# Hybrid encoder block on eight cores: another order of the first stages, loads that are held back, and value products that don't wait for their gelus

## What is computed

```
h = rms_norm(x);  lru_x, lru_gate, q, k, v = split(h @ w_in)      # five blocks of 512 columns
lru_x = causal_dwconv(lru_x, width 4)
r, i  = sigmoid(block_diag(lru_x)), sigmoid(block_diag(lru_x))
a     = exp(-8 r softplus(-lambda));  u = sqrt(1 - a^2) * (i * lru_x)
out_a = gelu(lru_gate) * scan(a, u)                               # scan along the positions
out_b = per head: rms_norm((softmax(q1 k1) - lam softmax(q2 k2)) @ v)   # block-causal, 4 heads
x     = x + concat(out_a, out_b) @ w_out
gate, val = split(rms_norm(x) @ ffn_w_up)                         # 2 x 3072 columns
x     = x + (gelu(causal_dwconv(gate, width 3)) * val) @ ffn_w_down
out   = rms_norm(x)
```

## Time and profile before

| | before |
|---|---|
| median of 3 runs | 1791.77 us (1791.51 to 1796.46) |
| the profiled execution | 1792.87 us, of which the slowest core's span is 1791.2 us |
| spans of the eight cores | 1778.5 to 1791.2 us |
| mean granted TensorE clock of the cores | 0.993 to 0.997 |
| PE busy, fills included | 1729.8 us, 97% of the span |
| DVE, ACT, POOL busy | 67%, 60%, 24% |
| fills in PE's list | 274 |

### The profile page before, as it was taken

One profiled execution on the slowest core, in us unless ns is written; L12 is line 12 of the kernel. 1 busy time (PEld: TensorE's weight loads), 2 busy tenths in 40 slices (PEclk: granted clock), 3 DMA queues, 4 the chain that ended last, 5 costly groups with the idle time before them and its releaser, 6 DMA issues.

```text
span 1791.2 us, 32281 instructions; the slowest of 8 cores (1778.5 to 1791.2 us)
## 1 busy us (share of the span) xinstructions
PE 1729.8 (97%) x9714; PEld 812.6 (45%) x9714; DVE 1193.2 (67%) x2049; ACT 1068.5 (60%) x1384; POOL 426.0 (24%) x631
## 2 busy tenths in 40 slices
PE   9988899999999999999999999999999999999997
PEld 4434344444444444444444444444444444454443
DVE  3498766562788585666986486866857378656844
ACT  6788764344877576654764376546766468742811
POOL 2272442210432131111511031111312033101300
PEclk9999999999999999999999999999999999999999
DMA  9980589773437835468558846585456644245633
GB/s 284 295 257 22 164 279 292 248 212 117 150 125 239 242 98 183 132 213 259 184 182 249 244 128 203 172 246 184 131 206 203 200 166 155 87 164 183 223 141 141
DMA packets 165417, 340.54 MB, mean 190 GB/s; under 512 B 73600, under 2 KB 73856, under 8 KB 165120
## 3 DMA queue, kind: packets, MB, share of 16 engines
q1 hardware_dynamic: 165248, 338.49, 59.7%
HBM read 267.14 MB, written 55.57 MB: 180 GB/s over the span
## 4 chain that ended last, share of the span: by engine, by line
PE 76%; DMA 6%; issue 6%; DVE 4%; ACT 4%; POOL 2%; SPq 1%; DVEq 0%; ACTq 0%; POOLq 0%
PE pb L865 40%; PE pb L883 24%; PE pb L1113 6%; PE pb L1080 4%; DMA slot<-x 3%; PE pb L718 1%; DMA KT<-w_up 1%; ACT raw L956 1%; DMA slot<-w_up 1%; ACT PT L1102 1%; POOL sm L851 1%; DMA Va<-w_down 1%; POOL raw L952 1%; DMA Va<-w_in 1%; DVE aT L973 0%
## 5 line engine op out<-in xcount | busy, mean ns | idle before, releaser
L865 PE MATMUL pb<-hT,slot 128*128 128x512 bf16 x3584 | 821.5, 379 | 8.5 <-ACT raw L956 4.8
L865 PEld LDWEIGHTS pb<-hT,slot 128*128 128x128 bf16 x3584 | 335.2, 98 | 421.5 <-issue 47.9
L1102 ACT ACTIVATE PT<-pb,prm 128x1024 bf16<-128x1024 f32 (+1 forms) x288 | 306.1, 1063 | 185.4 <-PE pb L1080 82.7
L883 PE MATMUL pb<-slot,aT 128*128 128x512 bf16 x1632 | 375.8, 380 | 3.5 <-DVE slot L1226 2.1
L883 PEld LDWEIGHTS pb<-slot,aT 128*128 128x128 bf16 x1632 | 154.5, 98 | 194.8 <-issue 20.2
L851 POOL TENSOR_TENSOR sm<-sm 128x1 f32<-128x1 f32 (+1 forms) x128 | 101.2, 793 | 552.6 <-DVE sm L848 550.7
L1226 DVE TENSOR_TENSOR slot<-pb,slot 128x512 f32<-128x512 f32 x192 | 130.7, 688 | 127.0 <-PE pb L883 126.2
L1216 DVE TENSOR_TENSOR aT<-pb,aT 128x512 bf16<-128x512 f32 x192 | 131.8, 688 | 119.9 <-PE pb L865 119.1
L1113 PEld LDWEIGHTS pb<-Va,PT 128*128 128x128 bf16 x2176 | 142.9, 98 | 75.7 <-issue 26.3
L1113 PE MATMUL pb<-Va,PT 128*128 128x129 bf16 x2176 | 171.3, 221 | 5.8 <-ACT PT L1102 5.5
L973 DVE SCALAR_TENSOR_TENSOR facc<-raw,prm,facc 128x512 f32<-128x512 f32 x192 | 144.2, 755 | 27.8 <-ACT facc L967 21.7
(11 more groups left out here) (133 smaller groups left out, 1671.6 us busy)
## 6 DMA issues: line engine op xcount, KB each, us to landing
slot<-wslab SPq DMA_DIRECT2D x326, 512.0 KB, 4.7
slot<-x SPq DMA_DIRECT2D x80, 512.0 KB, 6.9
wslab<-slot SPq DMA_DIRECT2D x50, 512.0 KB, 6.1
out<-slot SPq DMA_DIRECT2D x32, 512.0 KB, 5.1
x<-slot SPq DMA_DIRECT2D x24, 512.0 KB, 3.0
KT<-w_up SPq DMA_DIRECT2D x20, 512.0 KB, 8.0
Va<-w_up SPq DMA_DIRECT2D x20, 512.0 KB, 7.6
KT<-w_in SPq DMA_DIRECT2D x10, 512.0 KB, 9.7
```

Of the source, the lines that this page charges most:

```text
L865: last = e.matmul(bank(p), lhsT=w[:, kk, cc * 128:(cc + 1) * 128], rhs=src[:, hf * 4 + kk, :], start=(hf == 0 and kk == 0), stop=(hf == 1 ...
L883: last = e.matmul(bank(p), lhsT=src[:, k0 + hf * 4 + kk, t * 128:(t + 1) * 128], rhs=w[:, kk, :], start=(hf == 0 and kk == 0), stop=(hf == ...
L1102: op("act", act_us(2 * N, ptr=1), lambda e, s=s, pt=pt, N=N, h=h: e.activation(out=PT[:, pt.s, :, 0:N], in_=psum[:, s.s:s.s + 2, 0:N], fun ...
```

## The change

The first stages of groups 0 and 1 stand in another order: V, gate, LRU of group 0, Q, K instead of Q, K, V (stage A) with the gate and then the LRU. Stage A is split into `stage_Q`, `stage_K` and `stage_V`, and `pair` gives group 1's part of each its own offset in priority. The x tiles of group 1 are no longer loaded first but as part of stage N of group 1, behind (`behind=`) the second x tile of group 0. A new number `ahead` keeps a DMA from being placed in the list earlier than 6 modelled us before the DMA queue is free for it. The write-backs of the first weight slabs get a later priority. The value products of groups 0 and 7 lose their `after`, so that they may be placed ahead of the gelu (DVE's multiplication still reads the gelu's result). The numbers in the tables are new as well, those of the later groups included.

```diff
-        bw = 290e3
+        bw, ahead = 290e3, policy.get("ahead", 1e9)
...
+                    if n.dma and t < dma_free - ahead:
+                        t = dma_free - ahead
...
-        x0 = [[load_x(x_d, gi, t, ("XF", "X")[gi], pri=-8 + 2.12 * gi) for t in range(NT)] for gi in range(NP)]
+        x0 = [[load_x(x_d, 0, t, "XF", pri=-8 if t < 2 else -6.712) for t in range(NT)], []]
...
+                if gi == 1:
+                    x0[1].append(load_x(x_d, 1, t, "X", behind=behind))
...
-                p = mm_fm(sl, i, hT2, b_hT2, after=[b_aT[a]])
+                p = mm_fm(sl, i, hT2, b_hT2, after=[] if gi in (0, 7) else [b_aT[a]])
...
-                n.pri = period + f0 + (f1 - f0) * cum / tot
+                n.pri = period + f0 + (f1 - f0) * cum / tot + (0.6 if n.tag == "wb" and period < 2 else 0.0)
...
-        PR.update({'N0': (-6.483, -6.38), 'N1': (-6.091, -6.088), 'A': (-5.838, -5.301), 'G0': (-6.221, -6.266), 'L0': (-5.302, -4.564), 'L1': (-4.817, -3.395), 'B0': (-5.395, -4.633), 'B1': (-4.505, -3.624), 'C': (-4.474, -2.824)})
+        PR.update({'N0': (-6.384, -6.4), 'N1': (-6.361, -5.827), 'V': (-6.565, -6.864, 0.202), 'G': (-6.342, -6.558, 0.638), 'L0': (-6.114, -5.643), 'Q': (-6.112, -6.035, 0.428), 'K': (-5.9, -5.767, 0.741), 'L1': (-4.919, -3.721), 'B0': (-5.951, -5.545), 'B1': (-4.702, -3.5), 'C': (-4.573, -2.567)})
...
+        def pair(name, f, *args):
...
+                if n.grp == 1:
+                    n.pri += PR[name][2]
...
+        paced(0, *PR["N1"], stage_N, 1, [x0[0][1].ld])
+        pair("V", stage_V, *both)
+        pair("G", stage_G, both, (), "g0")
         paced(0, *PR["L0"], stage_L, 0)
+        pair("Q", stage_Q, *both)
+        pair("K", stage_K, *both)
...
-        S_.schedule({"attn": attn, "slots": slots, "warm": (idle, 0.8),
+        S_.schedule({"attn": attn, "slots": slots, "warm": (idle, 0.8), "ahead": 6.0,
```

More of the change, by code:

```diff
@@ L662, in build @@
         node({"sp": 0.1}, lambda e: e.dma_start(out=stg_v()[:, 128:nst], in_=stg_d[:, 128:nst]), reads=[stg_vt],
-             writes=[b_stg2], dma=(nst - 128) * 512, tag="stg", pri=-4.99)
+             writes=[b_stg2], dma=(nst - 128) * 512, tag="stg", pri=-6.472, behind=[x0[0][1].ld])
         node({"sp": 0.1}, lambda e: e.dma_start(out=prm[:, nsmall:npar], in_=par_d[:, nsmall:npar]), writes=[b_prmb],
-             dma=(npar - nsmall) * 512, tag="prm", pri=-4.5)
+             dma=(npar - nsmall) * 512, tag="prm", pri=-5.836, behind=[x0[0][1].ld])
         op("pool", 0.6, lambda e: e.memset(smv("mhalf"), -0.5), writes=[b_sm["mhalf"]])
@@ L888, in mm_tm @@
             for hf in range(2):
-                op("pe", MMC / 2, part(hf), reads=[slabs[hf][0]] + b_src, writes=[p], tag=tag,
+                p.pe = op("pe", MMC / 2, part(hf), reads=[slabs[hf][0]] + b_src, writes=[p], tag=tag,
                    after=after if hf == 0 else (), soft=list(soft) + [slabs[1][0].ld])
@@ L921, in stage_A, with stage_Q @@
                 op("pool", 0.6, lambda e: e.memset(Va[:, 12:16, :, 128:130], 1.0), writes=[b_stg1] + b_V[12:16])
-            stg = {2: [b_stg], 3: [b_stg1]}.get(gi, [])
-            sl = [load_slab(("in", 2, hf), "A", pr) for hf in range(2)]
+            stage_Q(gi)
+            stage_K(gi)
+            stage_V(gi)
+        def stage_Q(*gis):
+            S_.grp = gis[0]
+            sl = [load_slab(("in", 2, hf), "A", S_.pri) for hf in range(2)]
             for gi in gis:
                 S_.grp = gi
+                stg = claims(gi)
                 hT, b_hT, qT_, b_qT_ = place(gi)[:4]
@@ L929, in stage_A, with stage_K @@
                     evac(p, (lambda h=h: qT_()[:, h, :]) if gi == 1 else qT[:, h, :], b_qT_[h], scale=0.125, stg=stg)
-            S_.grp = 0
-            sl = [load_slab(("in", 3, hf), "A", pr) for hf in range(2)]
+        def stage_K(*gis):
+            S_.grp = gis[0]
+            sl = [load_slab(("in", 3, hf), "A", S_.pri) for hf in range(2)]
             for gi in gis:
                 S_.grp = gi
+                stg = claims(gi)
                 hT, b_hT = place(gi)[:2]
@@ L938, in stage_A, with stage_V @@
                     evac(p, KT[:, g, h, :], b_KT[h][g], stg=stg)
-            S_.grp = 0
-            sl = [load_slab(("in", 4, hf), "A", pr) for hf in range(2)]
+        def stage_V(*gis):
+            S_.grp = gis[0]
+            sl = [load_slab(("in", 4, hf), "A", S_.pri) for hf in range(2)]
             for gi in gis:
                 S_.grp = gi
+                stg = claims(gi)
                 hT, b_hT = place(gi)[:2]
@@ L1046, in stage_G @@
         def stage_G(gis, behind=(), visit=None):
-            pr = S_.pri
-            sl = [load_slab(("in", 1, hf), "F" if gis[0] == 0 else "A", pr) for hf in range(2)]
+            S_.grp = gis[0]
+            sl = [load_slab(("in", 1, hf), "F" if gis[0] == 0 else "A", S_.pri) for hf in range(2)]
             for gi, c in itertools.product(gis, range(4)):
@@ L1329, in build @@
         paced(0, *PR["N0"], stage_N, 0)
-        paced(0, *PR["N1"], stage_N, 1)
-        i0 = len(S_.nodes)
-        paced(0, *PR["A"], stage_A, *both)
-        for n in S_.nodes[i0:]:
-            if n.grp == 1:
-                n.pri += 0.772
-        i0 = len(S_.nodes)
-        paced(0, *PR["G0"], stage_G, both, (), "g0")
-        for n in S_.nodes[i0:]:
-            if n.grp == 1:
-                n.pri += 0.4
-                if n.visit:
-                    n.visit = "g1"
+        def pair(name, f, *args):
+            i0 = len(S_.nodes)
+            paced(0, *PR[name][:2], f, *args)
+            for n in S_.nodes[i0:]:
+                if n.grp == 1:
+                    n.pri += PR[name][2]
+                    if n.visit:
+                        n.visit = "g1"
@@ L1349, in build @@
         units = None
-        plan = [(0, {0: 0}, 'F', -4.706, -3.414), (1, {0: 0}, 'F', -3.522, -2.449), (0, {1: 8}, 'A', -0.324, 0.794), (1, {1: 0}, 'A', 0.153, 1.267), (2, {0: 8, 1: 0}, 'F', 1.084, 2.146)]
+        plan = [(0, {0: 0}, 'F', -4.409, -3.407), (1, {0: 0}, 'F', -3.416, -2.374), (0, {1: 8}, 'A', -0.008, 0.56), (1, {1: 0}, 'A', 0.535, 1), (2, {0: 8, 1: 0}, 'F', 0.855, 2.116)]
         for third, at, line, f0, f1 in plan:
@@ L1355, in build @@
             paced(0, 2, 2, stage_E, gi)
-        e_ = {2: -0.097, 3: -0.022, 4: 0.046, 5: -0.047, 6: 0.016, 7: 0.182}
+        e_ = {2: 0.037, 3: -0.022, 4: 0.127, 5: 0.089, 6: 0.016, 7: 0.159}
         if ngrp > NP:
-            paced(1 + -0.482, *FR["N"], stage_N, NP, [u1[0]])
-            paced(1 + -0.482, *FR["A"], stage_A, NP)
+            paced(1 + -0.44, *FR["N"], stage_N, NP, [u1[0]])
+            paced(1 + -0.44, *FR["A"], stage_A, NP)
         for gi in range(1, ngrp):
```

12 lines of the change are left out of this document (6 added, 6 removed).

## The result

The changed kernel takes 1775.27 us (median of 4 runs) beside 1792.04 for the kernel before; the ratio, which is that of the means of the runs, is 0.9894 with a 95% interval of 0.9874 to 0.9914. On another chip, later, it was 0.9875 (0.9858 to 0.9893). So the change is worth 1.1 to 1.3%, 17 to 22 us, where 8.7 were forecast: the direction was right, the forecast size about half of it.

The account below looks back on a forecast made before the run. PE, busy for 97% of the span, was taken as the bound, with gains from fills, idle time or clock. Terms +1.5 − 4 + 1 − 6.5 − 3.7 + 3.0 = −8.7 us took 1792.87 to 1784.2 (median 1783); range 1768 to 1798.

Parts of the forecast that it names:

- Start (A): Up to head 0's transposes: first product sooner, but six more fills at 0.254 us hand the gain back; +1.5 us.
- Heads (B): Between group 0's heads: fewer DVE instructions (67 for 72) and PE fills (71 for 88); −4 us, ends 0 and −6.
- Stage C (C): Stage C to first gate product: 24 fills instead of 18, but fewer DVE instructions; +1 us, ends −3 and +2.3.
- First values (D): Group 0's value products: 24 run ahead into three free banks, then wait for gelus; −6.5 us, ends −5.2 and −12.7.
- Elsewhere (E): Outside the other places, new tables of later groups: 12 more fills at 0.254 us; +3.0 us, ends 0 and +6.
- Last values (F): Last group: value products replace fills of 4.11 us, with all 8 banks free; −3.7 us, ends −4.1 and 0.
- late attention: Head 0, bounded by its own 33.8 us chain, has its transposes at 110.3; total 1798.5 us, chance 0.12.
- The waits did not stay: Rival that DVE and loads keep PE waiting, idle instead of on fills; +1.1 us, total 1793, chance 0.17.
- The clock fell: Rival that fewer fills with waits remaining lower PE's clock, 1.15 us a time, three times; total 1796.5, chance 0.03.
- more than forecast: The whole 12.69 us wait at the first values goes, heads gain 6, later fills cost nothing; −23.9 us, 1768, chance 0.14.

Follow-up runs that it names:

- last_ahead: The kernel before, with the wait for the gelus taken from the value products of group 7 alone; ratio 0.9994 (0.9978 to 1.0009).
- waits_back: The changed kernel, but the value products of groups 0 and 7 wait for their gelus again; ratio to the kernel before 0.9896 (0.9875 to 0.9917).

## Why the prediction was half right

In lost time, mean of the cores, against the terms of the sum:

- *Start (A)*, to head 0: forecast +1.5, measured +3.3. Priced by 6 more fills; PE idle besides them was left out. The landmarks came out: 18.13 for the first product (19.7), 76.41 for the first scores (76.5), 102.19 for head 0 (98.9).
- *Heads (B)*: forecast −4 (0 to −6), measured −7.1 on the mean core (−6.5 up to stage C), and 26.3 − 31.3 = −5.0 up to stage C on the slowest. The mechanism was right and the size too small. It was taken between the number of DVE's instructions, 7% fewer, and the fills; the instructions that left were long (two of four scans of 1.24 us, one of nine conv steps near 1 us), so DVE's busy time fell by 11%, and DVE was busy for 97% of what was left.
- *Stage C (C)*: forecast +1, measured −1.1 from head 3 to group 1's second head, and −0.1 in the stretch that was forecast, from stage C to the first gate product. Six more fills stood there, and no more was lost.
- *First values (D)*: forecast −6.5, measured −6.4. The number fits by luck. The picture was right in part: 24 value products (192.06 and 195.24) went ahead into three banks, and the next waited for DVE's multiplication until 207.66. But "So the gelus come perhaps 1 to 2 us sooner, not 10" was a step that failed: counted from the first gate product they came 5.6 us sooner with both changes, and 10.2 with the order alone. The release, which the prediction took as the cause, gave some of that back: without it the same stretch loses 1.4 us less.
- *Elsewhere (E)*: forecast +3, measured −7.2 from group 1's last head to unit 7200. This is the largest miss, 10 us. The step that failed was to price the new tables by 12 more fills (the lists have 57 instead of 46, so 11; the prediction's 61 and 49 are miscounted by a few). Undoing the numbers of `FR` alone costs 7.2 us with 6 fills more. The gain was mostly idle time that no fill covers, 17.6 us before and 12.0 now between units 1600 and 7200. The trace of before showed that idle time, as length less PE's busy time in the stretches of groups 2 to 7, and the prediction did not use it.
- *Last values (F)*: forecast −3.7, measured −3.7, shown by last_ahead alone.

The sum of the measured terms is −22.2 for the mean core; the slowest of eight, which sets the metric, kept 17.4 of it in the profiled run.

The rivals: late attention is out, since head 0's transposes came at 102.19, below 107.6, and its own chain took 25.8 us from the first scores, not 33.8. The waits did not stay between the heads and in groups 2 to 7; PE's idle time at the first values did (7.3 us of 7.4), as that rival had it, though its −2 for D lay outside D's own ends. The clock fell at the first values, to 0.92, which 28 value products show as some 1.5 us (7.53 instead of 28 x 0.216); it was 0.93 there before, but then it fell on fills (8 in 3.15 us), and cost 1.15 us at the down products behind them. The measured time lies between the forecast and "more than forecast", whose reason (the whole wait of D) was not the true one either.

Not settled: how the miss of 10 us in E splits on the mean core, since the new `FR` is worth 4.7 us in the kernel before and 7.2 in the changed one, and the other new tables were not tried alone.

## What to carry to other kernels

Don't price a reordered list by its count of filler work: fills stand where a planner expects a wait, cost nothing there (leaving out all 60.7 us of them made this kernel 4.5 us slower), and say nothing of the waits that it doesn't expect (waits_back has the 274 fills of the kernel before and is as fast as the changed kernel with 236). Take the lost time, length less work, stage by stage over the whole span, also where no fill stands. Where an in-order engine bounds a stretch, weigh what leaves it by duration, not by number. Two changes that clear the same thing out of the way do not add up. And a release that lets one engine run ahead can reorder the others: here it put a cast ahead of the gelus that the value products waited for.

## What the hardware showed beside this

Lost time at a given unit, as a mean of the same six cores, repeats from one chip to another within some 0.5 us up to unit 1600, where the times of whole executions differ by 0.3% and more (1792 and 1797 us for the same kernel before), so that for the first stages one profile tells single microseconds where three runs do not.
